# One decoder layer with a mixture of experts on one core: inverse by transposes, alternated attention heads, second norm and routing woven into their neighbours, and TensorE's expert loop rotated

## The reference, cut to what matters

```python
h = rmsnorm(x) * (1 + sc1) + sh1
# h @ w_in, causal conv, then
o_a = gated_delta_rule(q, k, v, beta, g, S0)      # 4 heads of 128: solves (I + M) uw = rhs, M strictly lower
o_b = gla_recurrence(q, k, v, log_a, S0)          # 4 heads, dk 64, dv 128
o_c = conformer convolution
merged = sum over branches of sigmoid(gate) * (branch @ w_branch)
x = x + gt1 * (merged @ w_out)
u = rmsnorm(x, norm_ffn_w) * (1 + sc2) + sh2
s = sigmoid(u @ router_w)                         # 64 experts, group-limited top 8 with a bias
for each block of 128 pairs (token, expert):      # pairs sorted by expert, 96 blocks here
    y = swiglu(u[rows], w_gate[e], w_up[e], w_down[e]) * gate   # 1024 -> 256 -> 1024
    routed[rows] += y
x = x + gt2 * (routed + swiglu(u, sh_w_gate, sh_w_up, sh_w_down))
```

## Time and profile before

| | |
|---|---|
| median of 3 runs | 3159.71 us (3156.04 to 3164.84) |
| the profiled execution | 3162.03 us, its span 3160.3 us |
| mean granted clock of TensorE | 0.942 |
| PE busy | 2927.3 us (93%) |
| DVE busy | 1107.8 us (35%) |
| ACT busy | 548.6 us (17%) |
| POOL busy | 749.2 us (24%) |
| DMA | 413.57 MB, mean 131 GB/s |

### The profile page before, as it was taken

The page is one execution under the profiler, slowest core; times in us unless marked ns, Lnnn a source line. Parts: engine busy times, 40 slices in busy tenths (PEclk is TensorE's granted clock), DMA queues, the critical chain, the costliest instruction groups (busy, mean ns, idle before and its releaser), DMA issues. The chain is left out here.

```text
span 3160.3 us, 31432 instructions
## 1 busy us (share of the span) xinstructions
PE 2927.3 (93%) x10624; PEld 1754.2 (56%) x10625; DVE 1107.8 (35%) x1642; ACT 548.6 (17%) x981; POOL 749.2 (24%) x986
## 2 busy tenths in 40 slices
PE   7998999999999899999999689599999989999994
...
GB/s 219 215 80 23 14 14 21 20 45 40 14 14 28 54 30 30 67 30 32 95 20 27 34 133 1 233 269 295 253 255 257 280 295 276 300 265 286 287 250 131
DMA packets 162802, 413.57 MB, mean 131 GB/s; under 512 B 17003, under 2 KB 104063, under 8 KB 134793
## 3 DMA queue, kind: packets, MB, share of 16 engines
q1 hardware_dynamic: 130449, 311.52, 27.5%
...
HBM read 339.65 MB, written 72.94 MB: 131 GB/s over the span
## 5 line engine op out<-in xcount | busy, mean ns | idle before, releaser
L2393 PE MATMUL ps<-big 128*128 x1536 | 696.4, 607 | 80.4 <-SPq L2316 33.1
L2393 PEld LDWEIGHTS ps<-big 128*128 128x128 f32 x1536 | 289.8, 194 | 421.5 <-issue 419.1
L2347 POOL DMA_INDIRECT big<-u_rows,big x384 | 370.1, 964 | 166.0 <-issue 83.7
L1711 PE MATMUL ps<-big 128*128 128x352 f32 x1152 | 348.8, 463 | 10.9 <-DMA big<-in_w_branch 10.9
L2404 PE MATMUL ps<-big 128*128 x768 | 345.3, 592 | 0.8 <-ACT big L2445 0.8
L1711 PEld LDWEIGHTS ps<-big 128*128 128x128 f32 x1152 | 220.7, 192 | 137.2 <-DMA big<-in_w_branch 12.6
L2474 DVE STREAM_TRANSPOSE big<-big 128x1024 f32<-128x1024 f32 x96 | 119.5, 1244 | 434.1 <-DMA big<-u_rows,big 434.1
L2404 PEld LDWEIGHTS ps<-big 128*128 128x128 f32 x768 | 145.8, 190 | 184.3 <-issue 184.3
L872 PE MATMUL ps<-big 128*128 128x352 f32 x576 | 202.1, 467 | 1.8 <-DMA big<-in_w_in 1.8
L2362 POOL DMA_INDIRECT y_rows<-big x96 | 155.9, 1624 | 173.4 <-DVE big L2489 89.9
L1284 PE MATMUL ps<-big 128*128 128x352 f32 x576 | 191.3, 479 | 1.9 <-ACT big L1373 1.3
...
## 6 DMA issues: line engine op xcount, KB each, us to landing
...
big<-u_rows,big POOLq DMA_INDIRECT x384
```

Of the source, the lines that this page charges most:

```text
L1711: ins = pe.matmul(ps[:, c, 0:CW], ring_g[:, q % 2, j, :], k.hT[:, j, c * CW:(c + 1) * CW], start=(j == 0), stop=(j == KT - 1))
L2347: g.indirect_dma_start(out=x_rows[:, u, x * 256:(x + 1) * 256], out_offset=None, in_=u_quarters, in_offset=bass.IndirectOffsetOnAxis(idx_i ...
L2393: ins = pe.matmul(ps[:, 2 + u, :].rearrange("p (g f) -> p g f", f=FF), xT[:, u, j, :], gate_up[:, j], start=(j == 0), stop=(j == KT - 1))
```

## The change

Five parts.

1. **delta_rule.** Below the last level X's correction is no longer a product of its own: Y is corrected, TensorE turns Y (4 transposes, banks 4 and 5) and ScalarE copies the result over X. A new fill point, levelx, stands behind; rows, turned1, turned0 and end give it their steps. The sum stays 32.
2. **gla_rule.** The products of the two heads of a pair alternate, so that one is of rows 0 to 63 and the next of rows 64 to 127; the fill of both heads follows. VectorE masks both and then sums both.
3. **The second norm** is no longer a function. In project_out ScalarE squares a tile as soon as it is added, VectorE adds the squares up, TensorE sums once; ScalarE takes the roots of one row, TensorE turns it to 9 columns, VectorE takes their reciprocals, TensorE spreads them, and VectorE, ScalarE and TensorE (logits) follow each other tile by tile. The router's and the shared expert's weights and the zeros to y_rows move into project_out.
4. **route.** The transposes of u are woven between the gate and up tiles, the placement's multiplication by the gate goes to POOL, the blocks of tile t are finished by VectorE behind the lanes of t + 1, four of eight shared down tiles stay in route, and SP loads expert 0's weights meanwhile.
5. **experts.** The other four shared down tiles stand first on TensorE; SP signals experts 0 to 2 as they land, before it waits for shared_added; TensorE's and VectorE's loops are rotated.

```diff
-FILL = dict(rows=2, products=1, turned1=3, turned0=5, first=2, level=1, levelxy=1, solved=2, new=2, end=3)
+FILL = dict(rows=1, products=1, turned1=2, turned0=4, first=2, level=1, levelxy=1, levelx=1, solved=2, new=2, end=2)
...
-                            if l < levels - 1:
-                                pe.matmul(ps[0:n, h, 0:n], XY[0:n, h, 1, 0:n], P1[0:n, h, 0:n], start=True, stop=True)
                             ins = pe.matmul(ps[0:n, h, n:2 * n], P1[0:n, h, 0:n], XY[0:n, h, 1, 0:n], start=True, stop=True)
                         ins.then_inc(level_filled, 1)
                     fill(filled_by[i, "levelxy", l])
+                    if l < levels - 1:
+                        for p in range(2):
+                            pe.wait_ge(level_done, level_at(i, l, p))
+                            for hh in range(2):
+                                h = 2 * p + hh
+                                ins = pe.transpose(ps[0:n, 4 + p, hh * n:(hh + 1) * n], XY[0:n, h, 1, 0:n], k.ident[0:n, 0:n])
+                            ins.then_inc(inv_filled, 1)
+                    fill(filled_by[i, "levelx", l])
...
+                        drain(filled_by[i, "levelxy", l])
+                        for p in range(2):
+                            act.wait_ge(inv_filled, inverse_at(i, l, p))
+                            act.activation(XY[0:n, 2 * p:2 * p + 2, 0, 0:n], ps[0:n, 4 + p, 0:2 * n].rearrange("p (h n) -> p h n", h=2),
+                                           ACT.Copy).then_inc(inv_done, 1)
...
+                        v.tensor_tensor(XY[0:n, hs, 1, 0:n], XY[0:n, hs, 1, 0:n], head_bank(p, n, 2 * n, n), ALU.subtract)\
+                         .then_inc(level_done, 1)
...
+                    pe.wait_ge(L_drained, 4 * i + 2 * p + 2)
+                    for l in range(levels + 1):
+                        for hh in range(2):
+                            r = slice(64 * hh, 64 * hh + 64)
+                            out = level_bank(hh, n)[:, l * n:(l + 1) * n]
+                            if l < levels:
+                                pe.matmul(out, Kf[p][r, l, 0:n], E[u][p][r, l, 0:n], start=True, stop=True)
+                            else:
+                                pe.matmul(out, k.gla[r, 2 + p, cols], k.gla[r, p, cols], start=True, stop=True).then_inc(L_filled, 1)
+                    fill(points[i, f"h{2 * p + 1}"])
...
+                    for step in (mask, gather):
+                        for hh in range(2):
+                            step(i, 2 * p + hh)
...
+            pe.wait_ge(gathered, KT - 2)
+            pe.wait_ge(drained, KT - 1)
+            for c in range(NCH):
+                pe.matmul(ps[:, SUMS[c], 0:CW], k.ones[:, :], acc[:, c * CW:(c + 1) * CW], start=True, stop=False)
+            pe.wait_ge(squared, KT)
+            for c in range(NCH):
+                ins = pe.matmul(ps[:, SUMS[c], 0:CW], k.ones[:, :], sq[:, (KT - 1) % 2, c * CW:(c + 1) * CW], start=False, stop=True)
+            ins.then_inc(summed, 1)
+            pe.wait_ge(rooted, 2)
+            for t in range(NT):
+                n = tokens_of(t)
+                ins = pe.matmul(ps[0:n, 6, t:t + 1], root[0:1, t * P:t * P + n], k.ones[0:1, 0:1], start=True, stop=True)
+            ins.then_inc(turned, 1)
+            pe.wait_ge(inverted, 2)
+            for t in range(NT):
+                n = tokens_of(t)
+                out = ps[:, 1 + t // 4, (t % 4) * P:(t % 4 + 1) * P] if t < 8 else ps[:, 7, 0:NS]
+                ins = pe.matmul(out, bcast(rstd[0:n, t:t + 1], P), k.ident[0:n, 0:n], start=True, stop=True)
+            ins.then_inc(spread, 1)
+            pe.wait_ge(router_loaded, 32)
+            pe.wait_ge(drained, KT)
+            pe.wait_ge(sampled, 1)
+            for j in range(KT):
+                pe.wait_ge(modulated, j + 1)
+                for c in range(NCH):
+                    ins = pe.matmul(ps[0:E_N, 3 + c, 0:CW], rw[:, j, :], k.hT[:, j, c * CW:(c + 1) * CW], start=(j == 0), stop=(j == KT - 1))
+            ins.then_inc(logits, 1)
...
+            for m in range(KT):
+                act.wait_ge(added, m + 1)
+                if m >= 3:
+                    act.wait_ge(gathered, m - 2)
+                act.activation(sq[:, m % 2, :] if m else acc[:, :], k.xT[:, m, :], ACT.Square).then_inc(squared, 1)
+            act.wait_ge(eps_ready, 1)
+            act.wait_ge(summed, 1)
+            act.activation(root[0:1, 0:2 * CW].rearrange("p (c w) -> p c w", c=2), ps[0:1, 6:8, 0:CW], ACT.Sqrt, scale=1.0 / D, bias=eps[0:1, :])\
+               .then_inc(rooted, 1)
+            act.activation(root[0:1, 2 * CW:T], ps[0:1, 0, 0:CW], ACT.Sqrt, scale=1.0 / D, bias=eps[0:1, :]).then_inc(rooted, 1)
+            for j in range(KT):
+                act.wait_ge(normed, j + 1)
+                act.activation(k.hT[:, j, 0:SEQ], k.hT[:, j, 0:SEQ], ACT.Identity, scale=k.mod[:, 4 * KT + j, 0:1],
+                               bias=k.mod[:, 3 * KT + j, 0:1]).then_inc(modulated, 1)
+            act.wait_ge(logits, 1)
+            act.activation(chunks(k.logits_T), ps[0:E_N, 3:6, 0:CW], ACT.Copy).then_inc(stopped, 1)
...
+                v.wait_ge(drained, m + 1)
                 s = samples(k.xT[:, m, :])
+                v.tensor_tensor(s, s, k.gate_tmp[:, m], ALU.add).then_inc(added, 1)
+                if m >= 2:
+                    v.wait_ge(squared, m)
+                    if m >= 3:
+                        v.wait_ge(gathered, m - 2)
+                    v.tensor_tensor(acc[:, :], acc[:, :], sq[:, (m - 1) % 2, :], ALU.add).then_inc(gathered, 1)
+            v.wait_ge(turned, 1)
+            v.reciprocal(rstd[:, 0:8], ps[:, 6, 0:8]).then_inc(inverted, 1)
+            v.reciprocal(rstd[0:NS, 8:9], ps[0:NS, 6, 8:9]).then_inc(inverted, 1)
+            v.wait_ge(spread, 1)
+            v.wait_ge(added, KT)
+            wide = ps[:, 1:3, :].rearrange("p a b -> p (a b)")
+            scale = k.mod[:, 4 * KT:5 * KT, 1:NSEQ]
+            s = k.hT[:, :, SEQ:T].rearrange("p k (s l) -> p k s l", l=SL)
+            for j in range(KT):
+                v.tensor_tensor(k.hT[:, j, 0:SEQ], k.xT[:, j, 0:SEQ], wide, ALU.mult).then_inc(normed, 1)
+                if j == 0:
+                    st(v.tensor_tensor(k.hT[:, :, SEQ:T], k.xT[:, :, SEQ:T], bcast(ps[:, 7, 0:NS].unsqueeze(1), KT, NS), ALU.mult))
+                    st(v.tensor_tensor(s, s, bcast(scale.unsqueeze(3), KT, SB, SL), ALU.mult))
+                    v.tensor_tensor(s, s, bcast(k.mod[:, 3 * KT:4 * KT, 1:NSEQ].unsqueeze(3), KT, SB, SL), ALU.add).then_inc(sampled, 1)
...
+                if t in (1, 3, 5):
+                    load_part(k, sp, 0, 0, t // 2)
...
+            hidden(0)
+            for t in range(NT):
+                g.wait_ge(q["lanes_ready"], t + 1)
+                blks = at_blk[t % 2]
+                g.tensor_tensor(blks[:, :, 1, :], blks[:, :, 0, :], bcast(slot_gate[:, t, :].unsqueeze(2), TOPK, NBLK), ALU.mult)\
+                 .then_inc(q["gated"], 1)
+                if t == 3:
+                    hidden(1)
...
+            def place(t):
+                pe.wait_ge(q["lanes_ready"], t + 1)
+                pe.wait_ge(q["blocks_ready"], t + 1)
+                for n in range(TOPK):
+                    ins = pe.matmul(ps[:, 6, 0:2 * NBLK], at_lane[t % 2][:, n, :],
+                                    at_blk[t % 2][:, n, :, :].rearrange("p a b -> p (a b)"),
+                                    start=(t == 0 and n == 0), stop=(t == NT - 1 and n == TOPK - 1))
+                ins.then_inc(q["placed"], 1)
+
+            for t in range(NT):
+                turn(t)
+                gate_up(t // 3, t % 3)
...
+            for t in range(NT):
+                place(t)
+                if t in (1, 2):
+                    gate_up(3, t)
+                m = t - (NT - SH_DOWN)
+                if m >= 0:
+                    if m == 0:
+                        pe.wait_ge(q["sh_hid_ready"], 2)
+                    pe.wait_ge(q["sh_drained"], m + 3)
+                    shared_down(k, pe, (3 * (m % 2), 3 * (m % 2) + 1, 3 * (m % 2) + 2), m).then_inc(q["sh_filled"], 1)
...
+            for t in range(NT + 1):
+                if t < NT:
+                    if t >= 2:
+                        v.wait_ge(q["placed"], t - 1)
+                    v.tensor_tensor(at_lane[t % 2][:, :, :], bcast(lane[:, t, :].unsqueeze(2), TOPK, P),
+                                    bcast(iota_f[:, 0:P].unsqueeze(1), TOPK, P), ALU.is_equal)
+                    v.tensor_tensor(at_blk[t % 2][:, :, 0, :], bcast(blk[:, t, :].unsqueeze(2), TOPK, NBLK),
+                                    bcast(iota_f.unsqueeze(1), TOPK, NBLK), ALU.is_equal).then_inc(q["lanes_ready"], 1)
+                if t:
+                    v.wait_ge(q["gated"], t)
+                    ones = at_blk[(t - 1) % 2][:, :, 0, :]
+                    v.tensor_scalar(ones, ones, tok[:, t - 1:t], None, ALU.mult).then_inc(q["blocks_ready"], 1)
...
+            for e in range(1, NW - 1):
                 load(e, e)
```

(39 more changed lines are left out.)

367 lines of the change are left out of this document (153 added, 214 removed).

## The result

The changed kernel takes 3043.26 us (median of 4 runs, 3037.95 to 3050.02), the kernel before 3158.40 us (4 runs); the ratio is 0.9634, 95% interval 0.9615 to 0.9654. The profiled execution has a span of 3038.3 us, 122.0 shorter than before. The forecast was 3070 with a range of 3035 to 3108, and rival A, 3047, comes nearest.

A forecast was written before the change was run, and what follows sets the result against it. TensorE's own work bounds delta_rule and gla_rule; other stretches have waits, and the expert loop has DMA 86% busy. Gains 15 + 10 + 22 + 15 + 19 + 9 = 90 us from 3162.0 give 3072, adjusted to 3070; range 3035 to 3108.

The forecast's parts named there:

- rival A: gla_rule: row halves run at once, loads and products both; 32 us shorter instead of 10, 3047 in all; chance 0.22.
- GLA heads: gla_rule: alternating the heads' row halves saves 10 us, within a possible nothing to 32.
- The row of 4-column products: Trace row used for gla_rule: 16 instructions streaming 4 columns still take 1.95 us, so 128-column loads set the pace.
- The row of column groups: Trace row used for gla_rule: 16 instructions in four column groups take 1.92 us against 7.25, so array parts run at once.
- The loop: Expert loop: earlier register loads and hidden rows before turning x save 9 us (0 to 25).
- The stall that I read in the earlier trace: Expert loop: hidden row late behind the turn of x, next product 1.88 us later; 27.5 us of this kind.
- two chains as long as TensorE's: Expert loop: POOL's gathers and scatter-adds and the weight loads set the pace, so most gain returns as other waits.
- Delta: delta_rule's inverse: transposes replace products, 18 us less, 3 lost to late copies; 15 us gain (6 to 18).
- Norm: Second norm, project_out's last product to the logits: 22 us gain (18 to 25), logits starting some 17 after.
- Routing: Routing stage: moved down tiles 14, most of 13 idle us gone, 10 back at uncovered gaps; 15 us gain (3 to 20).
- Beginning: Experts' beginning: earlier weights and readiness signals put the third block at 37 instead of 57; 19 us gain (13 to 22).
- Rival C: Expert loop: turning x behind the hidden row comes late, making the kernel slower, 3295 us; chance 0.03.

The follow-up runs named there:

- e1: The changed kernel with gla_rule's products of a pair going head after head again, merged fill kept: 3071.35 us, ratio 0.9717.
- e10: The kernel before with only the rotated TensorE and VectorE expert loops added: 3142.64 us, ratio 0.9949.
- e4: The changed kernel with the expert loop's old order: register loads behind the hidden row's wait, x turned before the hidden row: 3052.23 us, ratio 0.9660.
- e11: The changed kernel without loads of down weights from the fifth expert on (output wrong): 2988.81 us, ratio 0.9461.
- e7: The changed kernel with delta_rule's fill steps placed as before, none behind the inverse's transposes: 3072.01 us, ratio 0.9714.
- e2: The changed kernel with TensorE's register loads back behind the wait for the hidden row, VectorE's new order kept: 3047.44 us, ratio 0.9639.
- e5: The changed kernel with all four placement steps of a tile on VectorE in a row, none on GpSimd: 3030.85 us, ratio 0.9585.

## Why the prediction was right, and where its sizes were wrong

The time lies in the range, and every part that was forecast to gain did. The working holds up in part only. The sum is 27 us off the measured median, on the side of too little gain, for two reasons; they have the same sign, and only the width of the range took them in.

**GLA heads: mechanism undecided, size wrong.** The step that failed is "loads here are 128 wide, as in the slow row; I take 10". The row of 4-column products showed that a load sets the pace when all its rows are used; it said nothing of two loads into different rows. The row of column groups, which I weighed less, was the right one. The rule of the Trainium skill's page "TensorE: Matmul & The Clock Gate", section "Part 3: Packing small matmuls — row/col tiling", would have given 32; the trace after agrees (28 instructions in 1.83), and e1 shows that the alternation does it, with a part for the merged fill that I had not listed. TensorE's own work in the stage fell by 39 (319.3 to 280.3 between the same fills), 34 of it in these products, of which 29.3 arrived: its waits for VectorE grew by 9.7, before the fill's products that spread the inverted sums (L1238, 10.0 after and 5.1 before) and at two places more (2.7 and 2.1).

**The loop: mechanism right, size too low.** Forecast 9, measured 20.8 in the profile, 16 against the mean of seven loops, 16.5 in e10, about 10 in e4. The stall that I read in the earlier trace rows was the one: its 27.5 us vanish, and 3.1 of waits for the hidden row with them; 12.5 come back as late x and 4.8 as late weights. So "the greater part comes back as another wait" held, and TensorE's idle time fell by 13.4 (48.8 to 35.4). The other 7.4 are a term that the sum did not have: the same products take 1008.0 us before and 1000.6 after. Fewer waits mean fewer restarts (a block behind a short wait takes 7.13 us, not 7.03) and less time at half the clock (23.9 us before, 20.5 after), which is worth about 1.7; how the rest divides is open. Of up's whole group, 696.4 us before and 686.7 after, 4.6 lie ahead of the loop: the first two blocks took 10.05 and 8.60 before, at a granted clock of 0.78 from 2009.16 to 2030. And "two chains as long as TensorE's" was half right: in e11, with a third fewer loads of weights, GpSimd's chain keeps up (it waits 153.1 us for its own scatter-adds instead of 217.2), so the loads of the weights hold the loop and not that chain.

**Delta: right.** 18.2, the 18 that the four products were worth, with no late copy where I had put 3 for some; e7 shows how near that was. Had the cover failed, delta_rule would have been 3.8 longer than before, so my low end of 6 was too kind.

**Norm: right** (21.7 for 22), but in part by luck, since the clock helped: 0.91 in this stretch after and 0.80 before. In e2, with the same code, it was 0.76 and the stretch took 42.6, which would have made the term 17, below its low end of 18. The logits began 19.2 us after project_out's last product, not 17.

**Routing: right in size (14.0 for 15) and in place.** But two errors cancel. The sum had 14 for the moved down tiles, some 11 for the turns' idle time and 10 against for the three uncovered gaps. Measured, the tiles are 14.2; the turns 15, 10.2 of idle time and 4.7 of their own work, which the sum left out; and the placement takes 16.4 back, 12.3 of waits and 4.1 at the lower clock. The idle times before tiles 1, 4 and 5 are where it put them, but tile 4's extra 1.8 was GpSimd's queue (VectorE's lanes held up by the late multiplication), which the prediction had not followed. e5 shows that the move to GpSimd and the late finishing step cost 15 us of that stage: this part of the change works against it.

**Beginning: right** (21.9 for 19; third block at 36.7 after the stage's begin, forecast 37). It counted the first blocks at 7 us each without saying why, though the first took 10.05 before; the granted clock of the stretch was 1.00 after and 0.65 before, and some 4.6 of the gain is that. **Rival C** never came near: the turns behind hidden(n) cost 13.3 us in all.
